# A hybrid mixer's recurrence input: its third product on GpSimd, and the key-query products one projection piece later

## The chip, the cores and the metric

One core of a Trainium2 chip runs the whole program in one launch. The metric is the device time in microseconds (us). Five engines run their own queues of instructions and meet through semaphores: TensorE (PE, matmuls), VectorE (DVE), ScalarE (ACT), GpSimd (POOL) and SyncE (SP, which only issues loads and stores here).

## The reference, cut to what matters

The program is a chain of fourteen stages over a 256 x 1024 activation in float32. The second stage is the hybrid mixer, which projects its input once and runs a linear recurrence (LRU) and a chunked state-space part (SSD) on the results:

```python
def rg_lru(x, w_a, b_a, w_x, b_x, lam):
    r = sigmoid(block_diag_linear(x, w_a) + b_a)
    i = sigmoid(block_diag_linear(x, w_x) + b_x)
    log_a = -LRU_C * r * softplus(-lam)
    a = exp(log_a)
    u = sqrt(-expm1(2.0 * log_a)) * (i * x)
    # h[t] = a[t] * h[t-1] + u[t]

def ssd_chunked(x, dt, a, bm, cm):
    ...
    cb = einsum('bclgn,bcsgn->bgcls', cc, bc)
    y_diag = einsum('bgecls,bcsgep->bclgep', cb[:, :, None] * decay_in, xc)
    ...
```

`u` is a product of several factors over all 128 x 2048 elements. `cb` are the products of keys (`bm`) and queries (`cm`).

## The kernel before, in words

Activations lie transposed, feature on the partition, as eight tiles of 128 x 256. Weights come in pieces of 128 x 2048 float32. Each is loaded into `w_raw` by SP and split into a high part `w_hi` (ACT, line 625) and the rest `w_lo` (DVE, line 1262). PE multiplies three ways per tile: high by high, high by low, low by high (lines 2222 to 2224), 48 matmuls for a projection piece. Three buffers (`RING`) hold the pieces, so piece n+3 may overwrite piece n only when PE has used it.

The order of the hybrid stage is written out by hand in the string `HYBRID`. The functions `hybrid` of ACT, DVE and PE each walk the same string and emit what their engine has to do at each token, so a token that stands earlier is ahead in every queue. The tokens that matter:

- `in k`: projection piece k. PE projects it. ACT first makes the high part of piece k+2, then copies piece k out of its bank. DVE makes the low part of piece k+2, then may take one "ada slot": from `in11` on it folds half a tile of a later stage's modulation weights (`ada_half`, line 1411), which POOL's queue has loaded.
- `sqrt`, `mix0`: ACT's square root of `RC` (line 1059), then DVE's three products into `TI` (lines 1894, 1897, 1900), 128 x 2048 each. `scan0` (line 1905, eight scans) reads `TI`.
- `dt1` to `dt3`: the time steps of the SSD part. `dt2` is on ACT four short activations (lines 1074 to 1079), on DVE five short instructions (lines 1929 to 1939). In `dt3` PE transposes two rows (line 2704) and ACT copies them (lines 1083, 1084).
- `bcs0`, `xs k`: ACT's silu of keys and queries (line 1063) and of the values (line 1068).
- `cb0`: PE's eight instructions for the key-query products (lines 2680, 2681), and DVE's two masked copies out of the banks (line 1910), which raise `y_cb_read`.
- `turn0`: PE's sixteen transposes of the values (line 2689), which wait for `y_cb_read` because they use the same banks, and DVE's four scaled copies (line 1918).
- `dec k`, `head k`: decays and heads. PE's first `dec` (line 2717) waits for all four copies of `turn0`.

POOL issues the 128 loads of the modulation weights (`ada_wbuf`, line 595) in one loop, each behind a wait for the DVE fold that frees its buffer. The first 40 halves belong to the stage before, the next 16 to the hybrid stage.

Of the kernel before, what the change touches and what calls it, by code (L numbers as in the profile page):

```python
# [18 lines left out]
ALU = mybir.AluOpType  # L19
ACT = mybir.ActivationFunctionType  # L20
# [75 lines left out]
def mlstm_sequence():  # L96
# [3 lines left out]
    for h in range(MH):  # L100
# [3 lines left out]


HYBRID = """in0 in1 in2 lru0 in3 lru1 in4 lru2 in5 lru3 te0 dt0 in6 te1 dt1 in7 te2 in8 te3 in9 sqrt mix0 dt2 in10 bcs0 xs0
            in11 cb0 xs1 xs2 xs3 dt3 scan0 in12 turn0 in13 dec0 in14 head0 dec1 in15 head1 dec2 in16 head2 dec3 in17 head3
            dec4 row0 mul0 head4 dec5 row1 sum0 head5 dec6 row2 nrm0 head6 dec7 row3 head7 mul1 row4 sum1 nrm1 row5 row6
            row7"""

# [8 lines left out]
class Plan:  # L119
# [3 lines left out]
    def __init__(self, stages):  # L123
# [3 lines left out]
        for k, key in enumerate(stages):  # L127
# [29 lines left out]
ADA_WORK = {("ffn", 0): [(0, n) for n in range(8, 12)] + [(1, n) for n in range(12)] + [(2, n) for n in range(4)],  # L157
            ("hyb", 0): [(2, n) for n in range(4, 12)],
            ("ffn", 1): [(3, n) for n in range(12)] + [(5, n) for n in range(4)],
            ("ffn", 2): [(4, n) for n in range(12)] + [(5, n) for n in range(4, 8)],  # L160
            ("mlstm", 0): [(5, n) for n in range(8, 12)]}
# [4 lines left out]
def build(nc, a, out, stages):  # L166
# [13 lines left out]
    with ExitStack() as ctx:  # L180
# [17 lines left out]
        work = sb("work", [P, KT, T])  # L198
# [267 lines left out]
        TI = arena(6168, KT, T)  # L466
# [6 lines left out]
        RC = GL  # L473
# [75 lines left out]
        @block.gpsimd  # L549
        def _(pool):  # L550
            nchain = [0]

            def link(ins):
                nchain[0] += 1
                ins.then_inc(pool_chain, 1)
                pool.wait_ge(pool_chain, nchain[0])

            link(pool.memset(ident[:, :], 0.0))
            pool.memset(ones[:, :], 1.0).then_inc(const_ready, 1)
            pool.memset(eps_c[:, :], EPS).then_inc(const_ready, 1)  # L560
            pool.affine_select(out=ident[:, :], in_=ident[:, :], compare_op=ALU.not_equal, fill=1.0, base=0,
                               pattern=[[-1, P]], channel_multiplier=1).then_inc(const_ready, 1)


            for t in (causal, later):
                link(pool.memset(t[:, :], 1.0))
            for t in (turn, a_mask, c_mask):
                link(pool.memset(t[:, :], 0.0))
            halves = turn[:, :].rearrange("p (h c) -> p h c", h=2)

            def keep(view, op, fill, base, pattern, multiplier):
                link(pool.affine_select(out=view, in_=view, compare_op=op, fill=fill, base=base,
                                        pattern=pattern, channel_multiplier=multiplier))

            keep(causal[:, 0:256], ALU.is_ge, 0.0, 0, [[1, 256]], -1)
            keep(causal[:, 256:384], ALU.is_ge, 0.0, 0, [[1, P]], -1)
            keep(later[:, :], ALU.is_gt, 0.0, 0, [[-1, P]], 1)
            keep(halves[:, :, 0:32], ALU.not_equal, -1.0, -32, [[-64, 2], [-1, 32]], 1)
            keep(halves[:, :, 32:64], ALU.not_equal, 1.0, 0, [[-64, 2], [-1, 32]], 1)
            keep(a_mask[:, 0:256], ALU.is_ge, -1e30, 128, [[-1, 256]], 1)  # L580
            keep(a_mask[:, 256:384], ALU.is_ge, -1e30, 0, [[-1, P]], 1)
            keep(c_mask[:, 0:128], ALU.is_gt, -1e30, 0, [[1, P]], -1)
            keep(c_mask[:, 128:256], ALU.is_ge, -1e30, 0, [[-1, P]], 1)
            keep(c_mask[:, 256:384], ALU.is_ge, -1e30, 0, [[-1, P]], 1)
            link(pool.memset(blocks[:, :], 1.0))
            keep(blocks[:, :], ALU.is_ge, 0.0, 0, [[-4, 32]], 1)
            keep(blocks[:, :], ALU.is_ge, 0.0, 3, [[4, 32]], -1)
            pool.memset(sub_mark[:, :], 0.0).then_inc(masks_ready, 1)
            if plan.subs:
                pool.wait_ge(first_used, 2 * KT - 2)  # L590
                for i, piece in enumerate(ada_pieces):
                    for x in range(2):
                        if i:
                            pool.wait_ge(ada_chain, 2 * (i - 1) + x + 1)
                        pool.dma_start(ada_w[:, x, :], a["ada"][2 * (piece - 8) + x]).then_inc(ada_loaded[x], 16)  # L595


            for st in plan.steps:
                if st["key"][0] == "B":
                    for kind, u in sequence("B"):  # L600
                        if kind != "U":
                            continue
                        if u < 8:
                            pool.wait_ge(sp_ready, u + 1)
                            if u:
                                pool.wait_ge(r_ready, u)
                            pool.tensor_copy(sp_hi, sp).then_inc(sph_ready, 1)
# [3 lines left out]
        def _(act):  # L611
# [372 lines left out]
            def hybrid(st):  # L984
# [12 lines left out]
                def evacuate(k):  # L997
                    act.wait_ge(piece_used, n0 + k + 1)
                    b = io(n0 + k)
                    if k < 4:  # L1000
                        act.activation(XR[:, 2 * k:2 * k + 2, 3:T + 3], b, ACT.Copy)
                        for x in range(2):
                            t = 2 * k + x
                            ins = act.activation(XL[:, t, :], b[:, x, :], ACT.Identity, bias=col("lru_conv_b", t),
                                                 scale=col("lru_conv_w", 24 + t))
                    elif k < 6:
                        j = 2 * (k - 4)
                        act.activation(BCR[:, j:j + 2, 3:T + 3], b, ACT.Copy)
                        for x in range(2):
                            ins = act.activation(BC[:, j + x, :], b[:, x, :], ACT.Copy,  # L1010
                                                 scale=col("ssd_conv_w", 36 + 8 + j + x))
                    elif k < 10:
                        act.wait_ge(y_conv, 4)
                        j = 2 * (k - 6)
                        act.activation(XR[:, j:j + 2, 3:T + 3], b, ACT.Copy)
                        for x in range(2):
                            ins = act.activation(XS[:, j + x, :], b[:, x, :], ACT.Copy, scale=col("ssd_conv_w", 36 + j + x))
                    elif k < 14:
                        j = 2 * (k - 10)
                        ins = act.activation(ZG[:, j:j + 2, :], b, ACT.Silu)  # L1020
                    else:
                        j = 2 * (k - 14)
                        if k == 14:
                            act.wait_ge(y_mix, 1)
                        ins = act.activation(GL[:, j:j + 2, :], b, ACT.Copy if k < 17 else ACT.Gelu_apprx_tanh)
                    ins.then_inc(proj_ready, 1)

                for step, k in hybrid_sequence():
# [8 lines left out]
                    elif step == "lru":  # L1037
                        if k == 0:
                            act.wait_ge(y_lam, 1)
                        for t in (2 * k, 2 * k + 1):  # L1040
# [4 lines left out]
                                           scale=0.5).then_inc(y_th, 1)  # L1045
                    elif step == "te":
                        act.wait_ge(y_th, 2 * k + 2)
                        for t in (2 * k, 2 * k + 1):
                            ins = act.activation(RC[:, t, :], work[:, t, :], ACT.Tanh, bias=lam_4[:, t:t + 1],
                                                 scale=lam_4[:, t:t + 1])  # L1050
                        ins.then_inc(y_te, 1)
                        act.wait_ge(y_te, 2 * k + 1)
                        for t in (2 * k, 2 * k + 1):
                            ins = act.activation(work[:, t, :], work[:, t, :], ACT.Exp, bias=lam_2[:, t:t + 1],
                                                 scale=lam_2[:, t:t + 1])
                        ins.then_inc(y_te, 1)
                    elif step == "sqrt":
                        act.wait_ge(y_te, 8)
                        act.activation(RC, RC, ACT.Sqrt, scale=-1.0).then_inc(y_decay, 1)
                    elif step == "bcs":  # L1060
                        act.wait_ge(y_bc_conv, 2)
                        for t in range(4):
# [181 lines left out]
        def _(dve):  # L1244
            nchain = [0]

            def link(ins):
                nchain[0] += 1
                ins.then_inc(dve_chain, 1)
                return nchain[0]  # L1250

            def chained(n=None):
                dve.wait_ge(dve_chain, n or nchain[0])
# [573 lines left out]
            def hybrid(st):  # L1827
# [30 lines left out]
                for step, k in hybrid_sequence():  # L1858
# [31 lines left out]
                    elif step == "mix":  # L1890
# [3 lines left out]
                        link(dve.scalar_tensor_tensor(out=TI, in0=TI, scalar=1.0, in1=XL, op0=ALU.add, op1=ALU.mult))  # L1894
                        chained()
                        dve.wait_ge(y_decay, 1)
                        link(dve.scalar_tensor_tensor(out=TI, in0=work[:, :, :], scalar=1.0, in1=TI, op0=ALU.add,
                                                      op1=ALU.mult))
                        chained()
                        dve.scalar_tensor_tensor(out=TI, in0=RC, scalar=0.5, in1=TI, op0=ALU.mult,  # L1900
                                                 op1=ALU.mult).then_inc(y_mix, 1)
                    elif step == "scan":
                        dve.wait_ge(y_mix, 1)
                        for t in range(KT):
                            link(dve.tensor_tensor_scan(XL[:, t, :], work[:, t, :], TI[:, t, :], 0.0,
                                                        ALU.mult, ALU.add))
# [15 lines left out]
                    elif step == "dt":  # L1922
# [3 lines left out]
                        elif k == 2:  # L1926
# [3 lines left out]
                                                          op1=ALU.add))  # L1930
# [17 lines left out]
                    elif step == "head":  # L1948
                        dve.wait_ge(y_o, k + 1)
                        dve.scalar_tensor_tensor(out=XS[:, k, :], in0=XS[:, k, :], scalar=d_col[:, k:k + 1],  # L1950
                                                 in1=head_bank(st, k)[:, 0:T], op0=ALU.mult, op1=ALU.add).then_inc(y_y, 1)
# [1073 lines left out]
```

## Time and profile before

| what | value |
|---|---|
| time, median of 3 runs | 2405.68 us (2403.62 to 2410.78) |
| the profiled execution: time, span | 2406.78 us, 2404.7 us |
| PE busy | 2345.0 us, 98% |
| DVE busy | 1718.7 us, 71% |
| ACT busy | 1192.0 us, 50% |
| POOL busy | 80.7 us, 3% |
| chain that ended last | PE 80%, DVE 10%, ACT 4%, DMA 4%, issue 2% |

The span runs from the first to the last instruction of one profiled execution; 2.1 us of its time lie outside. The stage that changes lies at 230 to 410 us of the span. "Chain that ended last" is followed backwards from the last instruction through whatever released each step.

### The profile page before, as it was taken

What the parts mean: (1) busy time and instruction counts of PE and PEld (TensorE: products, weight loads), DVE (VectorE), ACT (ScalarE), POOL (GpSimd) and SP (SyncE); (2) the same over time, 40 slices, a digit from 0 to 9 for tenths busy, and PEclk for the clock granted to TensorE, in tenths of its full rate; (3) what the DMA queues carried; (4) which work ended last, traced back from release to release, by engine and by line L of the source; (5) the groups of instructions that cost most, each with busy time, mean ns of one, the idle gap of its engine ahead of it and who ended that gap; (6) DMA issues with size and microseconds to landing.
All of it is one profiled execution on the core that took longest, in us unless ns stands there. A gap on an engine that the chain in (4) does not pass through costs nothing.

```text
span 2404.7 us, 46561 instructions
## 1 busy us (share of the span) xinstructions
PE 2345.0 (98%) x19290; PEld 2259.5 (94%) x19290; DVE 1718.7 (71%) x2260; ACT 1192.0 (50%) x1489; POOL 80.7 (3%) x163
## 2 busy tenths in 40 slices
PE   6999999999999999999999999999999999999999
PEld 6999988999999989999988999899997899988999
DVE  7888788777877867655677666676667666677665
ACT  5335865334434655433556435654345633546434
POOL 1110000010010000000000000000000000000000
PEclk9999999999999999999999999999999999999999
DMA  8987465787788433455433554436542355443652
GB/s 342 326 314 264 158 217 204 279 295 267 273 297 289 175 135 111 172 194 191 172 123 124 208 192 158 148 116 209 193 175 79 123 204 193 156 153 111 210 192 105
DMA packets 75561, 471.62 MB, mean 196 GB/s; under 512 B 8632, under 2 KB 9144, under 8 KB 26808
## 3 DMA queue, kind: packets, MB, share of 16 engines
q1 hardware_dynamic: 56288, 400.79, 46.5%
q0 software_dynamic: 18432, 67.12, 7.9%
q10 hardware_dynamic: 728, 2.14, 0.3%
q8 instruction: 80, 1.31, 0.2%
q14 instruction: 33, 0.27, 0.0%
HBM read 468.96 MB, written 1.05 MB: 195 GB/s over the span
## 4 chain that ended last, share of the span: by engine, by line
PE 80%; DVE 10%; ACT 4%; DMA 4%; issue 2%; POOL 0%; ACTq 0%; DVEq 0%; POOLq 0%
PE bank L2222 23%; PE bank L2223 23%; PE bank L2224 23%; DVE w_lo L1262 2%; DMA ada_wbuf<-in_ada 2%; PE bank L2228 2%; DVE ada_wbuf L1411 2%; PE bank L2233 2%; PE bank L2229 2%; DMA ARENA<-in_first 1%; ACT w_hi L625 1%; PE bank L2450 1%; PE bank L2484 1%; ACT ARENA L916 0%; DVE ARENA L1734 0%
## 5 line engine op out<-in xcount | busy, mean ns | idle before, releaser
L1262 DVE TENSOR_TENSOR w_lo<-w_raw,w_hi 128x2048 fp32r<-128x2048 f32 x371 | 848.9, 2289 | 319.9 <-ACT w_hi L625 319.1
L625 ACT ACTIVATE w_hi<-w_raw 128x2048 fp32r<-128x2048 f32 x371 | 708.9, 1914 | 508.4 <-PE bank L2224 493.3
L2222 PE MATMUL bank<-h_hi,w_hi 128*128 128x256 f32 x3376 | 944.2, 280 | 1.5 <-DVE w_lo L1262 1.5
L2224 PE MATMUL bank<-h_hi,w_lo 128*128 128x256 f32 x3376 | 935.8, 277 | 0.0
L2223 PE MATMUL bank<-h_lo,w_hi 128*128 128x256 f32 x3376 | 935.8, 277 | 0.0
L2222 PEld LDWEIGHTS bank<-h_hi,w_hi 128*128 128x128 f32 x3376 | 634.7, 188 | 8.3 <-issue 5.1
L2223 PEld LDWEIGHTS bank<-h_lo,w_hi 128*128 128x128 f32 x3376 | 634.8, 188 | 3.5 <-issue 3.3
L2224 PEld LDWEIGHTS bank<-h_hi,w_lo 128*128 128x128 f32 x3376 | 634.6, 188 | 0.0
L2222 PE MATMUL bank<-d_hi,w_hi 128*128 128x256 f32 x1920 | 536.3, 279 | 4.1 <-DVE d_lo L1639 4.0
L2224 PE MATMUL bank<-d_hi,w_lo 128*128 128x256 f32 x1920 | 532.2, 277 | 0.0
L2223 PE MATMUL bank<-d_lo,w_hi 128*128 128x256 f32 x1920 | 532.1, 277 | 0.0
L2222 PEld LDWEIGHTS bank<-d_hi,w_hi 128*128 128x128 f32 x1920 | 360.6, 188 | 7.7 <-DVE d_lo L1639 5.5
L2223 PEld LDWEIGHTS bank<-d_lo,w_hi 128*128 128x128 f32 x1920 | 360.6, 188 | 0.5 <-issue 0.5
L2224 PEld LDWEIGHTS bank<-d_hi,w_lo 128*128 128x128 f32 x1920 | 360.5, 188 | 0.0
L1411 DVE CUSTOM_DVE_ANT_0 ada_wbuf<-ada_wbuf,c_rows 128x1024 f32<-128x1024 f32 x128 | 155.7, 1219 | 31.1 <-DMA ada_wbuf<-in_ada 31.1
L2228 PE MATMUL bank<-h_hi,w_hi 128*128 128x256 f32 x440 | 111.7, 286 | 3.2 <-ACT h_hi L676 2.8
L816 ACT ACTIVATE gate_s<-gate_s 128x512 f32<-128x512 f32 x44 | 27.9, 633 | 170.6 <-DVE gate_s L1572 170.6
L2229 PE MATMUL bank<-h_hi,w_lo 128*128 128x256 f32 x440 | 109.3, 281 | 0.0
L595 POOL DMA_DIRECT2D ada_wbuf<-in_ada x128 | 67.8, 530 | 786.0 <-DVE ada_sum L1411 756.2
L2228 PEld LDWEIGHTS bank<-h_hi,w_hi 128*128 128x128 f32 x440 | 83.5, 190 | 9.4 <-issue 7.7
L789 ACT ACTIVATE gate_s<-bank 128x512 f32<-128x512 f32 x40 | 24.0, 600 | 137.1 <-PE bank L2224 134.8
L1593 DVE CAST d_hi<-hid 128x512 fp32r<-128x512 f32 x88 | 37.5, 426 | 73.8 <-PE bank L2224 73.3
(407 smaller groups left out, 2271.9 us busy)
## 6 DMA issues: line engine op xcount, KB each, us to landing
w_raw<-in_ws SPq DMA_DIRECT2D x371, 1024.0 KB, 4.8
ada_wbuf<-in_ada POOLq DMA_DIRECT2D x128, 512.0 KB, 5.3
ARENA<-in_first SPq DMA_DIRECT2D x8, 1024.0 KB, 19.8
work<-in_x SPq DMA_DIRECT2D x1, 1024.0 KB, 11.3
ARENA<-in_wax ACTq DMA_DIRECT2D x1, 1024.0 KB, 4.8
out_y<-ARENA SPq DMA_DIRECT2D x4, 256.0 KB, 2.2
ARENA<-in_wg ACTq DMA_DIRECT2D x1, 768.0 KB
c_rows<-in_c SPq DMA_DIRECT2D x1, 512.0 KB, 4.9
```

The lines of the kernel that those rows point to most:

```text
L595: pool.dma_start(ada_w[:, x, :], a["ada"][2 * (piece - 8) + x]).then_inc(ada_loaded[x], 16)
L625: act.activation(w_hi[:, slot, :], w_raw[:, slot, :], ACT.Copy).then_inc(hi_ready, 1)
L816: act.activation(gate_s[:, :, :], gate_s[:, :, :], ACT.Silu).then_inc(silu_ready, 1)
L1262: dve.tensor_tensor(w_lo[:, s, :], w_raw[:, s, :], w_hi[:, s, :].bitcast(F32), ALU.subtract).then_inc(lo_ready, 1)
L1411: dve.tensor_tensor_reduce(out=w, in0=w, in1=c_rows[:, :], scale=1.0, scalar=0.0, op0=ALU.mult, op1=ALU.add, accum_out=dst).then_inc(ada_c ...
L1593: dve.tensor_copy(d_hi[:, buf, :, :], hid[:, :, :]).then_inc(dve_chain, 1)
L2222: pe.matmul(o, whi, xhi, start=start, stop=False, skip_group_check=True)
L2223: pe.matmul(o, whi, xlo, start=False, stop=False, skip_group_check=True)
L2224: return pe.matmul(o, wlo, xhi, start=False, stop=stop, skip_group_check=True)
L2228: pe.matmul(o, whi, xhi, start=start, stop=False, skip_group_check=True)
L2229: pe.matmul(o, wlo, xhi, start=False, stop=False, skip_group_check=True)
L2233: return pe.matmul(o, whi, xlo, start=False, stop=stop, skip_group_check=True)
```

## The change

The third product of `mix0` leaves DVE. Its factor 0.5 is folded into ACT's square root (scale -0.25 in place of -1.0), and the plain product `TI * RC` is issued on POOL, behind the 42nd load of the modulation weights. It waits for DVE's second product (`y_mix` at 1) and for the square root. The readers of `TI` (the scans) and the writer over `RC` (ACT at `in14`) now wait for `y_mix` at 2. In the order string, `cb0` moves from behind `in11` to behind `in12`; `dt3` and `scan0`, which stood between, now also come behind `in12`.

```diff
-            in11 cb0 xs1 xs2 xs3 dt3 scan0 in12 turn0 in13 dec0 in14 head0 dec1 in15 head1 dec2 in16 head2 dec3 in17 head3
+            in11 xs1 xs2 xs3 in12 cb0 dt3 scan0 turn0 in13 dec0 in14 head0 dec1 in15 head1 dec2 in16 head2 dec3 in17 head3
...
                         pool.dma_start(ada_w[:, x, :], a["ada"][2 * (piece - 8) + x]).then_inc(ada_loaded[x], 16)
+                    if i == len(ADA_WORK["ffn", 0]) and ("hyb", 0) in stages:
+                        pool.wait_ge(y_mix, 1)
+                        pool.wait_ge(y_decay, 1)
+                        pool.tensor_tensor(TI, TI, RC, ALU.mult).then_inc(y_mix, 1)
...
                         if k == 14:
-                            act.wait_ge(y_mix, 1)
+                            act.wait_ge(y_mix, 2)
...
-                        act.activation(RC, RC, ACT.Sqrt, scale=-1.0).then_inc(y_decay, 1)
+                        act.activation(RC, RC, ACT.Sqrt, scale=-0.25).then_inc(y_decay, 1)
...
                         dve.wait_ge(y_decay, 1)
-                        link(dve.scalar_tensor_tensor(out=TI, in0=work[:, :, :], scalar=1.0, in1=TI, op0=ALU.add,
-                                                      op1=ALU.mult))
-                        chained()
-                        dve.scalar_tensor_tensor(out=TI, in0=RC, scalar=0.5, in1=TI, op0=ALU.mult,
+                        dve.scalar_tensor_tensor(out=TI, in0=work[:, :, :], scalar=1.0, in1=TI, op0=ALU.add,
                                                  op1=ALU.mult).then_inc(y_mix, 1)
                     elif step == "scan":
-                        dve.wait_ge(y_mix, 1)
+                        dve.wait_ge(y_mix, 2)
```

On DVE, from the low parts of pieces 12 and 13 (line 1262 before, 1266 after) to the scaled copies of `turn0` (line 1918 before, 1919 after), the queue before reads:

```order
L1262 TENSOR_TENSOR w_lo<-w_raw,w_hi 128x2048 x2
L1411 ISA ada_wbuf,ada_sum<-ada_wbuf,c_rows 128x1024
L1411 ISA ada_sum 128x1
L1910 TENSOR_TENSOR ARENA<-bank,causal 128x384 x2
L1905 SCALAR_TENSOR_TENSOR ARENA<-work,ARENA 128x256 x8
L1262 TENSOR_TENSOR w_lo<-w_raw,w_hi 128x2048
L1411 ISA ada_wbuf,ada_sum<-ada_wbuf,c_rows 128x1024
L1411 ISA ada_sum 128x1
L1918 TENSOR_TENSOR ARENA<-bank,ARENA 128x512 x4
```

and after:

```order
L1266 TENSOR_TENSOR w_lo<-w_raw,w_hi 128x2048 x2
L1415 ISA ada_wbuf,ada_sum<-ada_wbuf,c_rows 128x1024
L1415 ISA ada_sum 128x1
L1266 TENSOR_TENSOR w_lo<-w_raw,w_hi 128x2048
L1415 ISA ada_wbuf,ada_sum<-ada_wbuf,c_rows 128x1024
L1415 ISA ada_sum 128x1
L1911 TENSOR_TENSOR ARENA<-bank,causal 128x384 x2
L1906 SCALAR_TENSOR_TENSOR ARENA<-work,ARENA 128x256 x8
L1919 TENSOR_TENSOR ARENA<-bank,ARENA 128x512 x4
```

The low part of piece 14 and a second fold now stand ahead of the masked copies (line 1910 before, 1911 after) and of the scans.

On PE, the queue before has the key-query products and `dt3`'s transposes between projection pieces 11 and 12, here with the last rows of piece 11 and the first of piece 12:

```order
L2223 MATMUL bank<-h_lo,w_hi 128x256
L2224 MATMUL bank<-h_hi,w_lo 128x256
L2680 MATMUL bank<-ARENA 128x256
L2681 MATMUL bank<-ARENA 128x128
L2680 MATMUL bank<-ARENA 128x256
L2681 MATMUL bank<-ARENA 128x128
L2704 MATMUL bank<-ident,hid 128x16 x2
L2704 MATMUL bank<-ident,rstd 128x16 x2
L2222 MATMUL bank<-h_hi,w_hi 128x256
```

and after, with the last rows of piece 12 ahead and the first of piece 13 behind:

```order
L2224 MATMUL bank<-h_lo,w_hi 128x256
L2225 MATMUL bank<-h_hi,w_lo 128x256
L2681 MATMUL bank<-ARENA 128x256
L2682 MATMUL bank<-ARENA 128x128
L2681 MATMUL bank<-ARENA 128x256
L2682 MATMUL bank<-ARENA 128x128
L2705 MATMUL bank<-ident,hid 128x16 x2
L2705 MATMUL bank<-ident,rstd 128x16 x2
L2690 MATMUL bank<-ident,ARENA 128x128 x16
L2223 MATMUL bank<-h_hi,w_hi 128x256
```

The products moved behind piece 12, and the transposes of `turn0` (line 2690 after) now follow them directly, where a whole projection piece stood between the two.

## Rows read from the trace of the kernel before

**Rows 1.** The page: busy times of the engines; the chain by engine.

```profile
PE 2345.0 (98%) x19290; PEld 2259.5 (94%) x19290; DVE 1718.7 (71%) x2260; ACT 1192.0 (50%) x1489; POOL 80.7 (3%) x163
...
PE 80%; DVE 10%; ACT 4%; DMA 4%; issue 2%; POOL 0%; ACTq 0%; DVEq 0%; POOLq 0%
```

**Rows 2.** PE's waits, 230 to 450 us: total us, times, longest.

```profile
PE bank L2222 <- DVE d_lo L1639: 2.7, 3, 2.0
PE bank L2680 <- ACT ARENA L1063: 1.9, 1, 1.9
...
PE bank L2717 <- DVE ARENA L1918: 1.5, 1, 1.5
```

**Rows 3.** Timeline of PE: start us, duration us, engine, line, instruction, [idle before, releaser].

```profile
301.60 0.70 PE L2680 MATMUL bank<-ARENA 128*128 128x256 f32 x2 [1.88 <-ACT ARENA L1063]
...
303.10 0.29 PE L2704 MATMUL bank<-ident,hid 16*128 16x16 f32 x2
...
304.87 0.36 PE L2222 MATMUL bank<-h_hi,w_hi 128*128 128x256 f32 x1 [1.35 <-DVE w_lo L1262]
...
310.39 1.91 PE L2689 MATMUL bank<-ident,ARENA 128*128 128x128 f32 x16
312.06 0.36 PE L2222 MATMUL bank<-h_hi,w_hi 128*128 128x256 f32 x1
...
319.45 0.50 PE L2717 MATMUL bank<-sp_r,pick_r 64*128 64x256 f32 x2 [1.50 <-DVE ARENA L1918]
```

**Rows 4.** Timeline of DVE over the same stretch.

```profile
295.61 2.29 DVE L1897 SCALAR_TENSOR_TENSOR ARENA<-work,ARENA 128x2048 f32<-128x2048 f32 x1
297.93 2.29 DVE L1900 SCALAR_TENSOR_TENSOR ARENA<-ARENA 128x2048 f32<-128x2048 f32 x1
300.14 0.40 DVE L1929 SCALAR_TENSOR_TENSOR hid<-hid,gate_s 16x256 f32<-16x256 f32 x1
...
300.96 0.68 DVE L1934 TENSOR_TENSOR_SCAN rstd<-ones,hid 16x256 f32<-16x256 f32 x1
...
302.43 4.49 DVE L1262 TENSOR_TENSOR w_lo<-w_raw,w_hi 128x2048 fp32r<-128x2048 f32 x2
306.84 1.22 DVE L1411 CUSTOM_DVE_ANT_0 ada_wbuf<-ada_wbuf,c_rows 128x1024 f32<-128x1024 f32 x1
...
307.99 1.02 DVE L1910 TENSOR_TENSOR ARENA<-bank,causal 128x384 f32<-128x384 f32 x2
308.92 4.76 DVE L1905 TENSOR_TENSOR_SCAN ARENA<-work,ARENA 128x256 f32<-128x256 f32 x8
313.59 2.27 DVE L1262 TENSOR_TENSOR w_lo<-w_raw,w_hi 128x2048 fp32r<-128x2048 f32 x1
...
316.92 2.48 DVE L1918 TENSOR_TENSOR ARENA<-bank,ARENA 128x512 f32<-128x512 f32 x4
```

**Rows 5.** Timeline of ACT over the same stretch, and its copy of piece 14.

```profile
296.06 0.18 ACT L1079 ACTIVATE ARENA<-ARENA 16x1 f32<-16x1 f32 x1
...
302.24 1.90 ACT L625 ACTIVATE w_hi<-w_raw 128x2048 fp32r<-128x2048 f32 x1
...
304.52 2.50 ACT L1068 ACTIVATE ARENA<-ARENA,cols 128x256 f32<-128x256 f32 x6
...
307.07 1.92 ACT L625 ACTIVATE w_hi<-w_raw 128x2048 fp32r<-128x2048 f32 x1
...
325.84 0.60 ACT L1025 ACTIVATE ARENA<-bank 128x512 f32<-128x512 f32 x1 [1.75 <-PE bank L2224]
```

**Rows 6.** POOL: its casts grouped, its first load in this stage, and a cast beside DVE.

```profile
L607 POOL CAST sp_r<-ARENA 128x768 fp32r<-128x768 f32 x8 | 6.6, 831 | 721.5 <-DVE ARENA L1709 721.5
...
308.36 0.54 POOL L595 DMA_DIRECT2D ada_wbuf<-in_ada  x1 [93.57 <-DVE ada_sum L1411]
...
1516.21 0.82 POOL L607 CAST sp_r<-ARENA 128x768 fp32r<-128x768 f32 x1 [653.74 <-DVE ARENA L1709]
...
1516.06 1.01 DVE L1716 SCALAR_TENSOR_TENSOR ARENA<-bank,ARENA 128x384 f32<-128x384 f32 x2
```

## The prediction

> **What bounds the kernel now.** I read the page first. TensorE is busy for 98% of the span and carries 80% of the chain [rows 1]. So a change elsewhere is worth only what it takes from or adds to PE's idle time, and the next view is PE's waits in the hybrid stage. Around the edit there are three: 1.88 us before the key-query products for ACT's silu, 1.35 before piece 12 for its low part from DVE, 1.50 before `dec0` for DVE's scaled copies [rows 2, 3]. Together 4.73 us, 0.2% of the time: this is all that the edit could win here. The third view is the timelines of the three engines from 296 to 320 us, where one asks what each has queued ahead of what PE waits for. DVE runs there without a gap: each row starts where the one before ends [rows 4].
>
> 0.3% is 7.2 us, about what a measurement of this kernel tells from no change; most of what follows is smaller.
>
> **What is removed from DVE.** The third product starts at 297.93 and `dt2` at 300.14 [rows 4]. Without it `dt2` starts at 297.93; ACT's last part of `dt2` is there, since it ended at 296.24 [rows 5]. `dt2` takes 302.43 - 300.14 = 2.29 us, so the low part of piece 12 starts at 300.22 in place of 302.43, 2.2 us earlier. PE began piece 12 2.44 us after that low part began (304.87 - 302.43 [rows 3, 4]), so now at 302.66. Piece 11 ended at 301.60 - 1.88 = 299.72 [rows 3]. PE thus waits 2.94 us in one piece. Before, it waited 1.88 + 1.35 there, with the products and `dt3` between; nothing is left now to put into the gap. Piece 12 takes 310.39 - 304.87 = 5.52 us and ends at 308.18.
>
> **What is moved on PE.** The products (303.10 - 301.60 = 1.50 us) and `dt3` (put at 0.4 us, two pairs like the one of 0.29) now follow piece 12. The products end at 309.68, `dt3` at 310.1, neither with a wait: the silu that the products need was there by 301.60. Next in the queue are the transposes of `turn0`, which wait until DVE has copied the products out. Before, DVE had all of piece 12 for that: the copies ended at 309.01 and the transposes began at 310.39 with no wait [rows 3, 4]. Now this wait lies open.
>
> **What is queued ahead of those copies on DVE.** By the order string: low part 13, a fold, low part 14, a fold. Steps from start to start are 2.2 us for a low part (two from 302.43 to 306.84) and 1.15 for a fold (306.84 to 307.99) [rows 4].
> - Low part 12: 300.22 to 302.43.
> - Low part 13 needs ACT's high part, which ends at 302.24 + 1.90 = 304.14 [rows 5]. ACT is in a row of work that the change doesn't shorten, so DVE idles 1.7 us. Low part 13 ends at 306.35, the fold at 307.50.
> - Low part 14 needs its high part, and ACT reaches that only behind the silus of the values, at 304.52 + 2.50 = 307.02; with 1.92 us it ends at 308.94 [rows 5]. DVE idles 1.4 us; low part 14 ends at 311.15, the fold at 312.30.
> - Copies: start 312.30, next start 0.93 later at 313.23, end 313.32. Scans 4.67 us (308.92 to 313.59) to 317.90. Scaled copies 2.48 us to 320.38 [rows 4].
>
> So DVE loses 3.1 us to waits for ACT and has won 2.2.
>
> **What PE pays.** The transposes start at 313.4, 3.3 us after `dt3` ended. They take 312.06 - 310.39 = 1.67 us, piece 13 takes 319.45 - 1.50 - 312.06 = 5.89 [rows 3]: its end is 320.94. DVE's scaled copies are there by then (320.38), so the old wait of 1.50 at `dec0` is gone. `dec0` starts at 320.94 where it was 319.45 [rows 3]: 1.5 us later. The same by waits: 2.94 + 3.3 = 6.2 us of idle PE in place of 4.73.
>
> **What carries the shift on.** From `dec0` the order is as before. ACT's copy of piece 13 and its `dec0` are 2.9 us later (317.95 to 320.94), but ACT had 1.75 us idle before its copy of piece 14 [rows 5], and piece 14 itself ends 1.5 later: 3.25 us cover 2.9. From there all shifts with PE, so 1.5 us stay to the end. The later waits of the stage are three for low parts of the stage's outputs, 2.7 us in all [rows 2]. I let them move along unchanged, since those outputs come from ACT and DVE work on what PE gives.
>
> **What is added on POOL.** One product of 128 x 2048. POOL has finished its 40 earlier loads and sits idle for 93.57 us up to 308.36, the 42nd included [rows 6], so the product starts as soon as the second product has ended, at about 298. The load queued behind it is not due before the fold at 307.5. No row shows this product. The nearest, POOL's cast, takes 831 ns for 768 elements, 1.08 ns each [rows 6]: 2.2 us for 2048 with one input, 4.4 if two inputs are read one after the other. Even 4.4 ends at 302.4, and the first reader is the scan at 313.2. The fold of 0.5 into the square root costs no instruction, and ACT's wait at piece 14 lies over 10 us later. So the product itself is put at nothing; DVE's and ACT's work up to 313 covers it.
>
> What it may cost is interference with DVE, whose instructions in this stretch mostly read two operands from SBUF. A cast on POOL ran from 1516.21 beside a DVE instruction of 1.01 us for two, whose other operand was in PSUM [rows 6], and this says nothing on two SBUF operands. Bounds: nothing, or DVE held for the whole product. I take nothing, since no row shows a hold, and keep the other as a rival.
>
> **Sum.** 0 (product) + 1.5 (PE later at `dec0`) on the profiled execution: 2406.8 + 1.5 = 2408.3. The median of the runs shown is 1.1 below that execution's 2406.78, so the forecast is 2405.7 + 1.5 = 2407.2 us.
>
> **Rivals.**
> - *DVE is held by POOL's product.* DVE's first short instruction of `dt2` runs to 298.33 (297.93 + 0.40), POOL then takes 4.4 us to 302.76, and the scan of `dt2`, due at 297.93 + 0.82 = 298.75, is 4.0 late [rows 4]. Low part 12 starts at 304.2, piece 12 at 306.7 to 312.2, products to 313.7, copies to 314.75, transposes to 316.5, piece 13 to 322.4: 2.9 us later than before, 2408.6. With 2.2 us for the product the delay is 1.8 and vanishes in DVE's wait for high part 13; the time is the forecast's. For it: almost every DVE instruction here reads twice. Against it: no row. The Trainium skill ("SBUF — State Buffer", section "Who interferes with whom") says that a DVE instruction with two SBUF inputs contends with a GpSimd instruction that reads SBUF, and that the later one blocks until the first is done; no run so far shows it. Its page "GPSIMD Engine Reference" (section "Elementwise — side-by-side cycle accounting") gives 4497 ns for a float32 addition of two tensors of this size; with it the delay would be 4.1 in place of 4.0.
> - *The product is kept waiting by DVE* and runs only when DVE itself waits for it at the scans, at 313.23: 4.4 us later the scans start, at 317.7, the scaled copies end at 324.8, `dec0` starts there, 5.4 us later than before: 2411.1. Against it: DVE has gaps from 302.4 and 307.5.
> - *Slower beyond the noise, by a slow product.* `dec0` would have to be 7.2 us late, at 326.65. Scans and scaled copies take 7.15, so the product would end at 319.5 and have lasted 21 us, 10 ns an element where the cast takes 1.08 [rows 6]. 2413 and above.
> - *A gain.* If ACT's high parts were early enough, DVE would run through: products out at 310.75, transposes to 312.5, piece 13 to 318.4, `dec0` 1.1 us earlier, 2404.6; the bound is 4.7 us, 2401.0. ACT's row of work from 302 to 309 [rows 5] speaks against it.
>
> **How the numbers follow.** Forecast 0.42; DVE held 0.33; product kept waiting 0.10; a small gain 0.10; slow product 0.03; something that I don't see 0.02. The range of 2403.0 to 2411.5 holds the first three whole and most of the fourth, with the scatter of the runs shown. Nearly all of it is within 0.3%: same 0.94. Slower beyond it takes the slow product and part of the kept one: 0.04. Faster 0.02, since all idle time at stake is less than 7.2 us.
>
> **What the profile after would show.** One wait of 2.9 us before piece 12; no wait before the products; one of 3.3 us before the transposes (line 2690), released by DVE's masked copies; none before `dec0`. On DVE gaps of 1.7 and 1.4 us for high parts. POOL's product from 298 for 2.2 to 4.4 us. If DVE is held, a hole of some 4 us in `dt2`, and piece 12 starts at 306.7. I am wrong if the wait before the transposes isn't there, or if the end moves by more than `dec0` does.

## The result: slower by a quarter of a per cent

The changed kernel takes 2413.7 us (median of 7 runs, 2408.3 to 2416.0) where the kernel before, run beside it, takes 2406.2 (7 runs). The ratio is 1.0025, with an interval of 1.0015 to 1.0035: 3.6 to 8.4 us more. (The two medians alone are 7.5 us apart, which lies inside that interval.) The forecast was 2407.2 with a range of 2403.0 to 2411.5, so the time lies above the range. In a second measurement (e8 below) the ratio was 1.0021 (1.0009 to 1.0033).

The profiled execution is the fastest of the seven (2408.3 us). Its span is 2406.5 us, 1.8 more than the span before, though the change costs more than that where it acts. It reached the end of PE's piece 11 2.5 us earlier, for reasons outside the change. Spells at half clock may be a part of them: the execution before has a lower granted clock between 20 and 30 us and between 40 and 50 (0.83), this one hasn't. So I compare stretches inside the stage, from the end of PE's projection piece 11 to the start of `dec0`: 319.45 - 299.72 = 19.7 us before [rows 3], and after 322.23 - (304.19 - 7.02) = 25.1 us.

PE's waits of the changed kernel from 230 to 450 us (its line numbers are one to four higher than before):

```profile
PE bank L2223 <- DVE w_lo L1266: 7.2, 2, 7.0
...
PE bank L2690 <- DVE ARENA L1911: 0.9, 1, 0.9
```

The three waits of [rows 2, 3] have become one of 7.0 us before piece 12 and one of 0.9 before the transposes. PE's timeline:

```profile
304.19 0.55 PE L2223 MATMUL bank<-h_hi,w_hi 128*128 128x256 f32 x1 [7.02 <-DVE w_lo L1266]
304.55 0.41 PE L2224 MATMUL bank<-h_lo,w_hi 128*128 128x256 f32 x1
...
312.03 0.59 PE L2681 MATMUL bank<-ARENA 128*128 128x256 f32 x2
...
314.70 1.94 PE L2690 MATMUL bank<-ident,ARENA 128*128 128x128 f32 x16 [0.86 <-DVE ARENA L1911]
...
322.23 0.49 PE L2718 MATMUL bank<-sp_r,pick_r 64*128 64x256 f32 x2
```

Piece 12 takes 312.03 - 304.19 = 7.8 us in place of 5.5. Of its 48 matmuls the 2nd to 21st last 0.41 us, where nearly all the others last 0.28. The view by stretches gives the granted clock (third figure from the end) for the wait, for the start of piece 12, and for the rest:

```profile
297.20:304.20 7.00, 0.01 (x1) 0.04 (x1) 6.87 (x6) 7.00 (x15) 2.90 (x1) 0.85 0.00 0
304.20:309.00 4.80, 4.80 (x23) 4.80 (x24) 4.80 (x4) 2.08 (x2) 0.60 (x1) 0.51 0.80 282
309.00:322.20 13.20, 12.34 (x104) 11.94 (x102) 10.37 (x18) 2.68 (x4) 0.53 (x1) 1.00 0.58 217
```

0.51 is the lower of the two levels, 1.2 GHz; PE had done nothing for 7 us before. Why the low part of piece 12 was so late stands in the timelines of DVE and POOL:

```profile
293.07 2.29 DVE L1901 SCALAR_TENSOR_TENSOR ARENA<-work,ARENA 128x2048 f32<-128x2048 f32 x1
295.28 0.41 DVE L1930 SCALAR_TENSOR_TENSOR hid<-hid,gate_s 16x256 f32<-16x256 f32 x1
295.72 4.53 DVE L1933 TENSOR_SCALAR hid<-hid,ARENA 16x256 f32<-16x256 f32 x1
...
301.75 4.49 DVE L1266 TENSOR_TENSOR w_lo<-w_raw,w_hi 128x2048 fp32r<-128x2048 f32 x2
...
313.54 1.02 DVE L1911 TENSOR_TENSOR ARENA<-bank,causal 128x384 f32<-128x384 f32 x2 [2.80 <-PE bank L2682]
...
295.44 4.66 POOL L599 TENSOR_TENSOR ARENA<-ARENA 128x2048 f32<-128x2048 f32 x1 [83.69 <-DVE ARENA L1901]
```

POOL's product runs from 295.44 to 300.10. A `TENSOR_SCALAR` of 256 elements, the second instruction of `dt2`, starts in that time and lasts until POOL is done: 4.53 us. Everything behind it on DVE moves. The masked copies (line 1911), which I had expected behind waits for ACT, now wait for PE: the products come so late that DVE's queue is empty.

### The profile page after: what moved, and what is told of

Read it like the earlier page. It is cut to its first block, busy times and chain, and to the rows that moved or that the text cites. A ratio compares the mean times of both kernels' runs of the same rounds, so it can differ in the third digit from the quotient of the medians.

```text
span 2406.5 us, 46562 instructions
## 1 busy us (share of the span) xinstructions
PE 2346.4 (98%) x19290; PEld 2261.1 (94%) x19290; DVE 1721.6 (72%) x2259; ACT 1192.2 (50%) x1489; POOL 85.4 (4%) x164
## 4 chain that ended last, share of the span: by engine, by line
PE 85%; DVE 7%; ACT 4%; issue 2%; DMA 1%; SPq 0%; ACTq 0%; DVEq 0%
PE bank L2223 25%; PE bank L2225 24%; PE bank L2224 24%; DVE w_lo L1266 2%; PE bank L2229 2%; PE bank L2234 2%; PE bank L2230 1%; ACT w_hi L629 1%; DMA ARENA<-in_first 1%; PE bank L2451 1%; PE bank L2485 1%; DVE ada_wbuf L1415 0%; DVE ARENA L1738 0%; DVE ARENA L1470 0%; DMA ada_wbuf<-in_ada 0%
## 6 DMA issues: line engine op xcount, KB each, us to landing
ARENA<-in_first SPq DMA_DIRECT2D x8, 1024.0 KB, 19.7
```

## The experiments

All times below are of the stretch from the end of piece 11 to `dec0`, unless they are called total. Theory: POOL's product holds DVE, PE then idles in one long stretch, and the clock falls. Rival: the new order alone does it.

**e1, the order alone.** The string as in the change, the product on DVE.

```diff
-            in11 cb0 xs1 xs2 xs3 dt3 scan0 in12 turn0 in13 dec0 in14 head0 dec1 in15 head1 dec2 in16 head2 dec3 in17 head3
+            in11 xs1 xs2 xs3 in12 cb0 dt3 scan0 turn0 in13 dec0 in14 head0 dec1 in15 head1 dec2 in16 head2 dec3 in17 head3
```

> Only the order string is changed; the third product stays on DVE (factor 0.5 there, square root as before). Measure: from the end of PE's piece 11 to the start of dec0 (line 2717 of the kernel before), 19.7 us before and 25.1 us with the whole change. Theory 1 (POOL's product holds DVE and is most of the loss): no hole in dt2 on DVE, low part 12 starts where it did, PE waits 5.2 us in one piece before piece 12, then about 1.1 us before the transposes for the masked copies; the stretch is about 21.2 us, 1.5 more than before. Rival (the order alone is the loss): PE waits 7 us or the clock falls all the same and the stretch is about 25 us. Total time: 2407 to 2408 by theory 1, 2411 or more by the rival.

PE's and DVE's timelines of e1 (its product at 296.27 on DVE lasts 2.29 us):

```profile
303.21 0.55 PE L2222 MATMUL bank<-h_hi,w_hi 128*128 128x256 f32 x1 [5.16 <-DVE w_lo L1262]
...
310.27 0.59 PE L2680 MATMUL bank<-ARENA 128*128 128x256 f32 x2
...
312.94 1.94 PE L2689 MATMUL bank<-ident,ARENA 128*128 128x128 f32 x16 [0.85 <-DVE ARENA L1910]
320.47 0.50 PE L2717 MATMUL bank<-sp_r,pick_r 64*128 64x256 f32 x2
...
298.92 0.34 DVE L1932 TENSOR_SCALAR hid<-hid,ARENA 16x256 f32<-16x256 f32 x1
...
311.78 1.02 DVE L1910 TENSOR_TENSOR ARENA<-bank,causal 128x384 f32<-128x384 f32 x2 [1.14 <-PE bank L2681]
```

The waits of 5.2 and 0.9 us are as the theory has them, and the `TENSOR_SCALAR` lasts 0.34. But the stretch is 320.47 - 298.05 = 22.4, not 21.2, as here too the clock fell: piece 12 takes 310.27 - 303.21 = 7.06 us, 1.3 more than the 5.75 that it takes at full clock in e5 below. So the order has a loss of its own of 2.7 us. Not all of the 1.3 reaches `dec0`: DVE waited 1.14 us for the products before its masked copies, so at full clock these could have started about 1.1 us earlier and no more. By this estimate 1.1 us of the loss is clock and 1.6 is the order itself. Total: ratio 1.0015 (1.0005 to 1.0025).

**e2, POOL's product alone.** The changed kernel with the old string.

```diff
-            in11 xs1 xs2 xs3 in12 cb0 dt3 scan0 turn0 in13 dec0 in14 head0 dec1 in15 head1 dec2 in16 head2 dec3 in17 head3
+            in11 cb0 xs1 xs2 xs3 dt3 scan0 in12 turn0 in13 dec0 in14 head0 dec1 in15 head1 dec2 in16 head2 dec3 in17 head3
```

> Only the product goes to POOL; the order string is that of before. Theory 1: one short instruction of dt2 on DVE lasts until POOL's product ends, 4.2 us longer than alone; low part 12 starts about 1.8 us later than before, PE still has the key-query products in that gap, so no idle stretch of PE is over 3.5 us and the clock stays; the stretch from the end of piece 11 to dec0 is about 21.5 us. Rival (POOL's product costs nothing of itself and the order does it): the stretch is at most 19.7 us.

Timelines of e2, PE, then DVE and POOL:

```profile
301.57 0.70 PE L2681 MATMUL bank<-ARENA 128*128 128x256 f32 x2 [1.89 <-ACT ARENA L1067]
...
302.93 0.64 PE L2682 MATMUL bank<-ARENA 128*128 128x128 f32 x2
...
306.71 0.55 PE L2223 MATMUL bank<-h_hi,w_hi 128*128 128x256 f32 x1 [2.58 <-DVE w_lo L1266]
...
322.67 0.50 PE L2718 MATMUL bank<-sp_r,pick_r 64*128 64x256 f32 x2
...
298.23 4.53 DVE L1933 TENSOR_SCALAR hid<-hid,ARENA 16x256 f32<-16x256 f32 x1
...
297.95 4.66 POOL L599 TENSOR_TENSOR ARENA<-ARENA 128x2048 f32<-128x2048 f32 x1 [83.20 <-DVE ARENA L1901]
```

The hold is the same to the hundredth. The stretch is 322.67 - 299.68 = 23.0 us, 3.3 over before. My expectation that the clock would stay was wrong, and the 3.5 us in it were no limit that any run had shown. It fell while the short products ran, behind a wait of only 1.9 us and ahead of the one of 2.6: their last pair takes 0.64 us where it took 0.39 before, and the granted clock from 302.4 on is 0.55. Piece 12 takes 8.5 us. Total: 1.0008 (0.9997 to 1.0019), by itself unclear. The rival is out for the hold and half right for the rest: each half of the change loses about 3 us here.

How much of e2's loss is clock can be estimated. DVE's scaled copies start at 318.75 (line 1919), 19.07 us behind piece 11 where it was 17.20 before, and DVE is never idle ahead of them; `dec0` before started 2.53 us after these copies did. At full clock the stretch would thus be 21.6 us, 1.9 over before. With the 1.6 of e1 this makes 3.5, near the 3.3 that e5 measures for the whole change at full clock.

**e3, POOL writes and doesn't read.** The product is replaced by two memsets of the same tile, so the products of the recurrence's input are left out.

```diff
-                        pool.tensor_tensor(TI, TI, RC, ALU.mult).then_inc(y_mix, 1)
+                        link(pool.memset(TI, 0.25))
+                        pool.memset(TI, 0.25).then_inc(y_mix, 1)
```

> The whole change, but POOL's product is replaced by two memsets of the same 128x2048 tile in a row, which write SBUF and read nothing. This leaves out the products of the recurrence's input. If it is POOL's reads that hold DVE: the memsets run 3 to 4 us beside DVE, dt2 has no hole, piece 12 starts 2.9 us after piece 11's end and the stretch to dec0 is 21.2 us. If any work of POOL in SBUF holds DVE: an instruction of dt2 lasts until the memsets end, and the stretch is 24 us or more.

POOL and DVE of e3:

```profile
301.91 1.83 POOL L599 MEMSET ARENA<- 128x2048 f32 x1 [83.53 <-DVE ARENA L1902]
303.79 1.83 POOL L600 MEMSET ARENA<- 128x2048 f32 x1
...
302.21 1.67 DVE L1934 TENSOR_SCALAR hid<-hid,ARENA 16x256 f32<-16x256 f32 x1
303.91 0.68 DVE L1936 TENSOR_TENSOR_SCAN rstd<-ones,hid 16x256 f32<-16x256 f32 x1
304.62 1.14 DVE L1939 CAST sp_r<-rstd 16x256 fp32r<-16x256 f32 x1
```

Neither answer alone. The `TENSOR_SCALAR` (0.34 us when POOL is idle) lasts until the first memset ends, the `CAST` (0.28) until the second ends; the scan, which starts inside the second, takes its usual 0.68. A write on POOL holds the first two kinds and not the scan. The stretch is 22.2 us, total 1.0015 (1.0002 to 1.0028).

**e4, who starts first.** `dt2` stands ahead of DVE's second product, so that low part 12 is next behind it.

```diff
                         link(dve.scalar_tensor_tensor(out=TI, in0=TI, scalar=1.0, in1=XL, op0=ALU.add, op1=ALU.mult))
+                        time_steps()
                         chained()
                         dve.wait_ge(y_decay, 1)
```

(`time_steps` holds the five instructions of `dt2`, which are gone from their old place.)

> The whole change, but DVE's five instructions of dt2 stand ahead of the second product, so that the next instruction behind that product is low part 12, which starts before POOL has woken up. If the one that starts first keeps the other out: low part 12 runs unheld (2.3 us), POOL's product starts only behind it or ends much later than 4.7 us after its release, and then low part 13 is held; PE waits about 3.6 us before piece 12 and about 3 to 5 us before the transposes; stretch about 23.4 us. If DVE always yields to POOL: low part 12 takes 4 to 7 us and piece 12 starts 7 us or more after piece 11. If there is no hold at all (the hole had another cause): stretch 21.2 us.

PE, DVE and POOL of e4:

```profile
306.36 0.36 PE L2225 MATMUL bank<-h_hi,w_hi 128*128 128x256 f32 x1 [3.58 <-DVE w_lo L1266]
...
318.38 3.26 PE L2692 MATMUL bank<-ident,ARENA 128*128 128x128 f32 x16 [2.94 <-DVE ARENA L1928]
...
327.23 0.50 PE L2720 MATMUL bank<-sp_r,pick_r 64*128 64x256 f32 x2
...
303.93 2.29 DVE L1266 TENSOR_TENSOR w_lo<-w_raw,w_hi 128x2048 fp32r<-128x2048 f32 x1
307.24 5.57 DVE L1266 TENSOR_TENSOR w_lo<-w_raw,w_hi 128x2048 fp32r<-128x2048 f32 x1 [1.03 <-ACT w_hi L629]
...
304.10 6.56 POOL L599 TENSOR_TENSOR ARENA<-ARENA 128x2048 f32<-128x2048 f32 x1 [86.25 <-DVE ARENA L1918]
```

Low part 12 began 0.17 us before POOL and ran its usual 2.29. POOL's row lasts 6.56, 1.9 longer than in the other runs. It ends at 310.66, and low part 13, begun at 307.24, takes 2.29 and 3.3 more. So the first to start keeps the other out, whichever it is. The hold moved to where it hurts PE later, before the transposes (2.9 us). The stretch is 327.23 - (306.36 - 3.58) = 24.5 us, total 1.0015 (1.0005 to 1.0025). Part of the stretch is clock again: piece 12 takes 7.3 us, with a granted clock of 0.51 from 307.4 to 310.8, and the transposes last 3.26 us in place of 1.94, at 0.55.

**e5, PE kept busy in the gap.** The whole change, with extra matmuls before piece 12 into a bank that nobody reads.

```diff
+                            if k == 12:
+                                pe.wait_ge(y_th, 8)
+                                for _ in range(56):
+                                    pe.matmul(PS[3][:, 0:T], h_hi[:, 0, 0:P], h_hi[:, 0, :], start=True, stop=True,
+                                              skip_group_check=True)
```

> The whole change, with 56 extra matmuls of 256 columns on PE between pieces 11 and 12, where PE stood idle for 7.0 us; they write a bank that nobody reads and take 56 times 0.114 = 6.4 us. If it is the idle stretch that lets the clock fall, the granted clock stays at full level through piece 12 (no row of 0.41 us), and the stretch from the end of piece 11 to dec0 is 25.1 less about 2.2 us, some 22.9. If the fall has another cause, 22 matmuls at half speed stand there as before and the stretch is 25 us.

PE of e5, then the granted clock over the gap and piece 12:

```profile
311.15 0.38 PE L2223 MATMUL bank<-h_hi,w_hi 128*128 128x256 f32 x1 [0.30 <-DVE w_lo L1266]
316.90 0.59 PE L2686 MATMUL bank<-ARENA 128*128 128x256 f32 x2
...
327.10 0.49 PE L2723 MATMUL bank<-sp_r,pick_r 64*128 64x256 f32 x2
...
304.10:311.10 7.00, 6.75 (x57) 6.54 (x55) 6.87 (x6) 7.00 (x15) 3.05 (x1) 1.00 0.00 0
311.10:316.90 5.80, 5.75 (x48) 5.75 (x49) 5.80 (x5) 2.17 (x2) 0.60 (x1) 1.00 0.75 290
```

The clock stays, piece 12 takes 5.75 us, and the stretch from 304.14 is 23.0 in place of 25.1, as expected. POOL's hold is there as before. So the clock cost 2.1 us of the stretch, and this is shown by a run that differs in nothing else. Total: 1.0018 (1.0007 to 1.0029) against 1.0021 of e8 on the same chip: too little to tell in the total.

**e6, the product in four.** Each part of 128x512 is issued behind the one before.

```diff
-                        pool.tensor_tensor(TI, TI, RC, ALU.mult).then_inc(y_mix, 1)
+                        for j in range(4):
+                            part = TI[:, 2 * j:2 * j + 2, :]
+                            ins = pool.tensor_tensor(part, part, RC[:, 2 * j:2 * j + 2, :], ALU.mult)
+                            if j < 3:
+                                link(ins)
+                        ins.then_inc(y_mix, 1)
```

> The whole change, with POOL's product cut into four of 128x512, each behind the end of the one before. If the hold is for one instruction of POOL at a time, DVE's waiting instruction gets in between two parts: the hole in dt2 is cut into several of at most 1.3 us, and low part 12 starts somewhere between 1 and 4 us late. If POOL keeps DVE out for as long as it has work, one hole of over 4.5 us as in the changed kernel. Stretch 22 to 25 us.

DVE of e6:

```profile
299.05 1.27 DVE L1938 TENSOR_SCALAR hid<-hid,ARENA 16x256 f32<-16x256 f32 x1
300.36 1.71 DVE L1940 TENSOR_TENSOR_SCAN rstd<-ones,hid 16x256 f32<-16x256 f32 x1
302.10 1.18 DVE L1943 CAST sp_r<-rstd 16x256 fp32r<-16x256 f32 x1
303.31 1.45 DVE L1945 TENSOR_TENSOR sp_r<-rstd,sp_r 16x256 fp32r<-16x256 f32 x1
```

The hold is for one instruction of POOL at a time, but `dt2` is a chain of short instructions and each meets the next part. Their extra times are 0.93, 1.03, 0.90 and 1.04, together 3.9 us. Nothing is won: stretch 325.58 - 300.50 = 25.1 us, total 1.0023 (1.0014 to 1.0033). It also shows that the scan is held by a product, though not by a memset.

**e8, the changed kernel again.**

> The changed kernel once more, beside the others on the same chip: a hole of 4.2 us in dt2 and an idle stretch of 7.0 us on PE stand there again, followed by matmuls at half clock; 25 us from the end of piece 11 to dec0; total 0.2 to 0.25% over the kernel before.

```profile
305.64 0.55 PE L2223 MATMUL bank<-h_hi,w_hi 128*128 128x256 f32 x1 [7.02 <-DVE w_lo L1266]
...
323.64 0.50 PE L2718 MATMUL bank<-sp_r,pick_r 64*128 64x256 f32 x2
```

The wait is the same to the hundredth, half clock follows it, and the stretch is 323.64 - 298.62 = 25.0 us.

**e7, e9 and e10, a version that should beat both.** From the kernel before, all on DVE: the third product behind low part 12, the scaled copies ahead of low part 14, the folds of `in11` and `in12` moved to later slots. e9 is e7 again; e10 has the folds where they were.

```diff
-             "hyb": [0] * 11 + [1] * 7 + [2] * 1 + [1] * 7, "mlstm": [0] * 8 + [2] * 4}
+             "hyb": [0] * 13 + [1] * 5 + [2] * 3 + [1] * 5, "mlstm": [0] * 8 + [2] * 4}
...
                     if step == "in":
-                        lo_ahead(n0 + k + 2)
+                        if k != 12:
+                            lo_ahead(n0 + k + 2)
+                        if k == 10:
+                            chained(mixed)
+                            dve.scalar_tensor_tensor(out=TI, in0=RC, scalar=0.5, in1=TI, op0=ALU.mult,
+                                                     op1=ALU.mult).then_inc(y_mix, 1)
...
                                               ALU.mult).then_inc(y_xc, 1)
+                        lo_ahead(n0 + 14)
```

> The kernel before with DVE's queue reordered and nothing on POOL: the third product stands behind low part 12, the two folds of in11 and in12 go to later slots, the scaled copies stand ahead of low part 14. If DVE's queue is what sets dec0, piece 12 starts 1.35 us earlier, dec0 about 2.2 us earlier: stretch 17.5 us in place of 19.7, total 0.1% under the kernel before. If ACT or something else sets it: stretch 19.5 us or more, total unchanged. A risk is that the two later folds lengthen the end of the stage.

> The reordered kernel (nothing on POOL, DVE's queue reordered) once more. If the 2.7 us that it won in the stretch before dec0 reach the end, total 0.1% under the kernel before (ratio about 0.999). If they are given back later in the stage, the total is that of before (1.000) again, and the profile shows dec0 to the first work of the next stage longer than the 88.8 us of the kernel before.

> The reordered kernel with the two folds back in their old slots at in11 and in12 (third product behind low part 12, scaled copies ahead of low part 14, as there). The folds stand ahead of the masked copies and, one of them, of the scaled copies: DVE's queue up to dec0 is 1.15 to 2.3 us longer, so the stretch should be 18.2 to 19.4 us in place of 17.0. If the later folds of the reordered kernel cost at the end of the stage, this one wins there what it loses here, and both totals are alike.

PE of e7, one of its waits between 352 and 368 us, and DVE in two later rows of the stage:

```profile
300.48 0.70 PE L2684 MATMUL bank<-ARENA 128*128 128x256 f32 x2 [1.88 <-ACT ARENA L1063]
...
315.60 0.50 PE L2721 MATMUL bank<-sp_r,pick_r 64*128 64x256 f32 x2
...
PE bank L2643 <- DVE ARENA L1950: 1.4, 1, 1.4
...
364.70 1.22 DVE L1411 CUSTOM_DVE_ANT_0 ada_wbuf<-ada_wbuf,c_rows 128x1024 f32<-128x1024 f32 x1
...
365.84 1.22 DVE L1411 CUSTOM_DVE_ANT_0 ada_wbuf<-ada_wbuf,c_rows 128x1024 f32<-128x1024 f32 x1
...
366.99 0.48 DVE L1954 SCALAR_TENSOR_TENSOR ARENA<-ARENA,bank 128x256 f32<-128x256 f32 x1
...
376.12 0.48 DVE L1954 SCALAR_TENSOR_TENSOR ARENA<-ARENA,bank 128x256 f32<-128x256 f32 x1
```

The stretch is 315.60 - 298.60 = 17.0 us, 2.7 less than before, and 16.8 in e9. The total doesn't move: 1.0005 (0.9994 to 1.0016) and 1.000 (0.999 to 1.0009). The stage gives it back, as the second case of e9's expectation had it. From `dec0` to DVE's first update at the stage's end (line 1381) it takes 403.14 - 315.60 = 87.5 us in e7 and 88.3 in e9, where it was 404.32 - 319.45 = 84.9. (The 88.8 us in e9's expectation are counted to another point and aren't to be compared with these.) Most of it is put down to the folds: in `row1` and `row2` two now stand in a row, 1.15 us more each, 2.3 of the 2.6 us. From one `head` to the next DVE takes 10.49 and 9.13 us (356.50, 366.99, 376.12), in the kernel before 9.33 and 7.98 (360.04, 369.37, 377.35). PE waits 1.4 us there, where its one wait for that DVE instruction was 0.2 before. e10 was to check this.

e10 has its folds at the old places and gives the time back elsewhere. PE of e10, `dec0` and piece 14:

```profile
317.86 0.49 PE L2721 MATMUL bank<-sp_r,pick_r 64*128 64x256 f32 x2 [0.35 <-DVE ARENA L1921]
320.15 0.36 PE L2226 MATMUL bank<-h_hi,w_hi 128*128 128x256 f32 x1 [1.79 <-DVE w_lo L1262]
```

Its stretch is 317.86 - 300.44 = 17.4 us, better than expected, since DVE had 1.8 us to spare in e7 (its scaled copies end at 313.82, `dec0` starts at 315.60). But right behind `dec0` PE waits 1.8 us for low part 14, which I had put behind the copies. The clock falls there too: from 321.1 to 324.5 it is 0.51, and piece 14 takes 327.50 - 320.15 = 7.35 us where e7's takes 5.8. From `dec0` to the first update it takes 406.88 - 317.86 = 89.0 us; without these 1.8 and 1.5 us it would be 85.7, about what it is in the kernels whose folds weren't moved. This fits the folds as the cause in e7 and e9, but it is an argument and not a clean test. The total of e10 is 0.9999 (0.9989 to 1.0009).

None of the versions tried beats the kernel before. Where they put the work, DVE had no time to spare. It has some elsewhere in the stage: it is busy for 150 of the 180 us from 230 to 410, and for only 5.3 of the 10 from 260 to 270. No run tried to use that.

## Why the prediction was wrong, by its steps

- **"I take nothing, since no row shows a hold."** This step failed. The hold is real and the size was that of my rival: the product lasts 4.66 us (4.4 by two casts' rate), DVE loses 4.2. The absence of a row was no evidence, since no row before had POOL reading SBUF beside a DVE instruction that could be held. I gave this rival 0.33. Its rule, in the Trainium skill's page "SBUF — State Buffer", section "Who interferes with whom", agrees with the runs: the first to start wins (e4), and of the instructions with two SBUF inputs a product holds the scan (1.71 us in e6) and low part 13 (5.57 in e4), while a memset doesn't hold the scan (0.68 in e3). But the rival had the hold fall on the scan of `dt2`, for its two inputs, and it fell on the `TENSOR_SCALAR` before it, which reads one tensor and one scalar per partition. This kind is held by a mere write as well. The same section of the Trainium skill says that copies, casts and `tensor_scalar` can take both ports, and then contend with one input; the `TENSOR_SCALAR` and `CAST` of e3 agree, at 1.67 and 1.14 us.
- **The rival's sum** had PE wait 306.7 - 299.7 = 7.0 us before piece 12, as measured (7.02), and put `dec0` 2.9 us late. Without the clock, e5 measured 23.0 - 19.7 = 3.3. That leaves 25.1 - 23.0 = 2.1 us, which neither sum had.
- **The missing term is TensorE's clock.** I added waits and never asked what one wait in place of three does. 7.0 us without a matmul, and the start of piece 12 ran at 1.2 GHz. Even the forecast's own course had a longer unbroken wait than the kernel before. In e1, with nothing on POOL, 5.2 us of idle time were enough.
- **The order's loss** was forecast as 1.5 us. e1 gives 22.4 - 19.7 = 2.7, of which by the estimate there 1.1 is clock: 1.6 without it. The mechanism was the one named, DVE's copies and the transposes behind each other. The waits for ACT that I had put into DVE's queue shrank, since low part 12 came later than forecast (by 2.2 us in e1, by 4.1 in the changed kernel): e1 has one of 0.8 us for a high part, the changed kernel none. And in the changed kernel the wait before the transposes was 0.9 us and not 3.3, because by then the products, not DVE's queue, were late.
- **"1.5 us stay to the end"**: a shift at `dec0` does carry through. From `dec0` to the next stage's first update it is 407.22 - 322.23 = 85.0 us, before 84.9, and 84.8 to 85.5 in e1 to e6 and e8. From the end of piece 11 to the first projection of the next stage it is 416.24 - 297.17 = 119.1 us against 412.00 - 299.72 = 112.3, so 6.8 us, with another spell at half clock behind the update. e8 has this spell too, e1, e3 and e5 haven't, so it isn't shown to come of the change. The measured 0.25% is 6.0 us.
- **The range** ended at the case in which the product is kept waiting, 2411.1. It had no case in which a hold and the clock add up: with the measured 5.4 us at `dec0` the forecast's own sum gives 2405.7 + 5.4 = 2411.1, just inside its upper end. What lies between that and 2413.7 is not settled; the 6.8 - 5.4 = 1.4 us behind `dec0` and the scatter of the runs are candidates.
- **No gain beyond the noise**: right. What PE waits for there is mixed, and e7 shows that even 2.7 us won before `dec0` don't arrive at the end.

## What to carry to other kernels

Work given to GpSimd beside a DVE that is busy may not be taken off DVE at all: here 2.3 us of DVE work became 4.7 us of GpSimd work, and DVE stood still for 4.2 of them, in an instruction of sixteen partitions that has nothing to do with it. Cutting the work in four didn't help, and letting DVE start first only moved the hold. Before moving such work, ask which DVE instruction will start while GpSimd runs, and who waits behind that one. When waits of the matmul engine are merged, by moving the small work that lay between them, price the one long gap with the clock behind it and not as the sum of the short ones. A short gap is no safeguard either: behind 1.9 us the clock stayed in the kernel before and fell in e2.

## What the runs showed of the hardware

- A GpSimd product of two float32 tensors, 128x2048, lasts 4.66 us; DVE does it in 2.29. A memset of that size on GpSimd lasts 1.83.
- A held instruction of 16x256 ends within 0.2 us of GpSimd's end in the changed kernel and in e3: 0.34 us of work became 4.53. The held low part in e4, 128x2048, ends 2.15 us after it, about the 2.29 that it takes alone.
- The granted clock fell to the lower level behind idle stretches of 7.0 (the changed kernel and e8), 6.7 (e6), 5.2 (e1) and 5.0 us (e3). Behind 3.6 us in e4, 1.9 in e2 and 1.8 in e10 it fell about 1 us after the matmuls had begun again. It stayed in the kernel before, in e7 and in e9 behind the same 1.9. So a short wait may cost a spell of it or not. The spells behind these gaps made a projection piece, 5.5 to 5.8 us at full clock, last 7.0 (e3) to 8.5 us (e2). Other spells stand at other places in each execution; they may be part of why single runs of the kernel before lie between 2402 and 2414 us, which wasn't tried.
